# Scores of the next pair at the end of a pair's projection, and values turned in shared visits, in a decoder layer on one core

## The reference, cut to what matters

```python
def dilated_mixture_attention(h, w_in, w_out):
    qkv = (h @ w_in).reshape(B, S, 3, DSW_GROUPS, DSW_HEADS, DSW_HEAD_DIM)
    for g, (window, dilation) in enumerate(((128, 1), (512, 4), (2048, 16))):
        o, lse = dilated_window_attention(qkv[:, :, 0, g], qkv[:, :, 1, g], qkv[:, :, 2, g], window, dilation)
        outs.append(o); lses.append(lse)
    weights = jax.nn.softmax(jnp.stack(lses, axis=0), axis=0)
    o = jnp.sum(weights[..., None] * jnp.stack(outs, axis=0), axis=0)
    return o.reshape(B, S, D_MODEL).astype(h.dtype) @ w_out
```

## Time and profile before

| | us |
|---|---|
| median of 3 runs | 953.76 (953.18 to 954.54) |
| profiled execution, its own time | 953.11 |
| its span, first to last instruction | 951.3 |
| PE busy in the span | 927.2 (97%) |
| DVE, ACT busy | 577.5 (61%), 446.5 (47%) |

### The profile page before, as it was taken

One profiled execution on the slowest core, in us unless ns is written; L12 is line 12 of the kernel. 1 busy time (PEld: TensorE's weight loads), 2 busy tenths in 40 slices (PEclk: granted clock), 3 DMA queues, 4 the chain that ended last, 5 costly groups with the idle time before them and its releaser, 6 DMA issues.

```text
span 951.3 us, 16326 instructions
## 1 busy us (share of the span) xinstructions
PE 927.2 (97%) x5828; PEld 798.7 (84%) x5828; DVE 577.5 (61%) x1269; ACT 446.5 (47%) x804; POOL 51.2 (5%) x75
## 2 busy tenths in 40 slices
PE   7999999999999999999999899999999999999996
PEld 6688888888888888888888689889999999888884
DVE  3445655636736557357374757788888888733325
ACT  7244534435444445363443454655665665523222
POOL 2000000000000000000000001411211111000000
PEclk9999999999999999999999999999999999999998
DMA  9866341443324324334143112367877886432302
GB/s 305 252 184 170 111 133 47 131 133 110 122 76 132 110 69 128 112 110 154 45 133 96 38 53 81 104 155 176 185 184 180 178 196 146 156 110 89 110 1 89
DMA packets 166516, 121.19 MB, mean 127 GB/s; under 512 B 4662, under 2 KB 149198, under 8 KB 166478
## 3 DMA queue, kind: packets, MB, share of 16 engines
q1 hardware_dynamic: 161088, 111.17, 38.9%
q0 software_dynamic: 5184, 9.44, 6.6%
q10 hardware_dynamic: 206, 0.08, 0.0%
HBM read 109.13 MB, written 2.10 MB: 117 GB/s over the span
## 4 chain that ended last, share of the span: by engine, by line
PE 89%; DVE 5%; ACT 2%; POOL 1%; DMA 1%; issue 1%; SPq 1%; DVEq 0%; ACTq 0%
PE bank L778 14%; PE bank L780 13%; PE bank L779 13%; PE bank L983 7%; PE bank L986 7%; PE bank L985 7%; PE bank L1032 4%; PE bank L1033 4%; PE bank L1034 4%; PE bank L860 3%; PE bank L836 3%; PE bank L803 1%; PE bank L796 1%; PE bank L818 1%; PE bank L869 1%; PE bank L871 1%
## 5 line engine op out<-in xcount | busy, mean ns | idle before, releaser
L1379 DVE TENSOR_TENSOR wl<-raw,wh 128x1024 fp32r<-128x1024 f32 (+1 forms) x127 | 150.2, 1183 | 166.2 <-ACT wh L1090 165.6
L778 PE MATMUL bank<-hh,wl 128*128 128x512 f32 x544 | 218.1, 401 | 0.0
L780 PE MATMUL bank<-hl,wh 128*128 128x512 f32 x544 | 212.4, 390 | 0.0
L779 PE MATMUL bank<-hh,wh 128*128 128x512 f32 x544 | 212.0, 390 | 0.0
L1090 ACT ACTIVATE wh<-raw 128x1024 fp32r<-128x1024 f32 (+1 forms) x127 | 130.4, 1028 | 61.4 <-PE bank L1034 50.2
L778 PEld LDWEIGHTS bank<-hh,wl 128*128 128x128 f32 x544 | 102.3, 188 | 23.9 <-issue 3.5
L780 PEld LDWEIGHTS bank<-hl,wh 128*128 128x128 f32 x544 | 102.1, 188 | 22.2
L779 PEld LDWEIGHTS bank<-hh,wh 128*128 128x128 f32 x544 | 102.3, 188 | 19.5
L1161 ACT ACTIVATE probs<-probs,nmax 128x256 f32<-128x256 f32 (+1 forms) x128 | 61.8, 484 | 67.5 <-DVE nmax L1455 67.5
L983 PE MATMUL bank<-th,wl 128*128 128x256 f32 x304 | 86.2, 284 | 1.6 <-ACT p_copy L1247 0.9
L986 PE MATMUL bank<-tl,wh 128*128 128x256 f32 x304 | 86.0, 283 | 0.0
(11 more groups left out here) (220 smaller groups left out, 1609.2 us busy)
## 6 DMA issues: line engine op xcount, KB each, us to landing
raw<-in_attn_w_in SPq DMA_DIRECT2D x72, 512.0 KB, 3.8
ada_raw<-in_w_ada SPq DMA_DIRECT2D x16, 1024.0 KB, 6.1
raw<-in_ffn_w_up SPq DMA_DIRECT2D x25, 512.0 KB, 4.2
sums<-in_ffn_w_up SPq DMA_DIRECT2D x36, 256.0 KB, 3.4
raw<-in_ffn_w_down SPq DMA_DIRECT2D x17, 512.0 KB, 3.3
sums<-raw POOLq DMA_DIRECT2D x27, 256.0 KB, 4.8
ada<-in_w_ada SPq DMA_DIRECT2D x16, 256.0 KB, 6.6
raw<-in_attn_w_out SPq DMA_DIRECT2D x8, 512.0 KB, 3.6
```

The lines of the kernel that those rows point to most:

```text
L778: nc.tensor.matmul(bank[:], wl[:, slot, t], xh[:, t], start=(t == 0), stop=False)
L779: nc.tensor.matmul(bank[:], wh[:, slot, t], xh[:, t], start=False, stop=False)
L780: last = nc.tensor.matmul(bank[:], wh[:, slot, t], xl[:, t], start=False, stop=(t == KT - 1))
L1379: nc.vector.tensor_tensor(dst, src, high.bitcast(F32), ALU.subtract).then_inc(done, 1)
```

## The change

Four things are moved; no arithmetic is added or taken away.

- Scores 0 and 1 of a pair go from h 0 of the body that attends to it to h 16 of the body that projects it, behind the values of the pair before. Their masks and exponentials go to h 16 and 17. On ACT the copy `o_a` goes ahead of them.
- Values: turn 0 and turn 1 at h 4, just ahead of scores 2 and 3, turn 2 at h 12 ahead of the sum. The first pair keeps its own table.
- In body 8 only scores 2 and 3 are left, at h 1 instead of 4, with their masks and exponentials at h 1 and 2.
- The filling steps of body 8 are spread anew: 3 and 18 at h 0 and 1 instead of 5 and 15 at h 0 and 4, and 3 instead of 4 at h 16.

The semaphore of scores 0 asks only for strips up to 4 of its pair, that of scores 2 for all.

```diff
-        SCORE_AT = {0: (0, 1), 4: (2, 3)}
-        MASK_AT = {0: 0, 1: 1, 4: 2, 5: 3}
-        TURN_V_AT = {3: 0, 5: 1, 7: 2}
+        SCORE_AT = {4: (2, 3)}
+        SCORE_LAST = {1: (2, 3)}
+        SCORE_AHEAD = {16: (0, 1)}
+        MASK_AT = {4: 2, 5: 3}
+        MASK_LAST = {1: 2, 2: 3}
+        MASK_AHEAD = {16: 0, 17: 1}
+        TURN_V_AT = {4: (0, 1), 12: (2,)}
...
-        FILL_AT = {0: 5, 4: 15, 12: 1, 13: 1, 14: 1, 15: 1, 16: 4}
+        FILL_AT = {0: 3, 1: 18, 12: 1, 13: 1, 14: 1, 15: 1, 16: 3}
...
                 if d == 0:
+                    pe.wait_ge(strip_taken, STRIPS * (n - 1) + GROUPS + 2)
+                if d == 2:
                     pe.wait_ge(strip_taken, STRIPS * n)
...
+                    if project:
+                        for d in SCORE_AHEAD.get(h, ()):
+                            make_scores(n + 1, par, d)
...
+                    if project and h in MASK_AHEAD:
+                        if attend and h == 16:
+                            copy_output(n)
+                        exponentials(n + 1, MASK_AHEAD[h])
                 if attend:
-                    act.wait_ge(pv_done, 4 * n)
-                    nc.scalar.activation(o_a[:].rearrange("p (b j r) -> p b j r", b=NT, r=4),
-                                         o_acc[0][:].rearrange("p (b r j) -> p b j r", b=NT, r=4),
-                                         ACT.Copy).then_inc(oa_copied, 1)
+                    if not project:
+                        copy_output(n)
                     act.wait_ge(o_summed, n + 1)
...
+                    if project and h in MASK_AHEAD:
+                        mask_scores(n + 1, MASK_AHEAD[h])
```

More of the change, by code:

```diff
@@ L259, in decoder_layer @@
         HALVES = 2 * STRIPS
-        TURN_V_FIRST = {8: 0, 9: 1, 10: 2}
+        TURN_V_FIRST = {8: (0,), 9: (1,), 10: (2,)}
         ADA_READ_FIRST = {4: 0, 5: 1, 6: 2, 7: 3, 12: 4, 13: 5, 14: 6, 15: 7}
         ADA_FIRST = 17
-        FILL_AT = {0: 5, 4: 15, 12: 1, 13: 1, 14: 1, 15: 1, 16: 4}
+        FILL_AT = {0: 3, 1: 18, 12: 1, 13: 1, 14: 1, 15: 1, 16: 3}
         OUT_AHEAD = 4
@@ L905, in body @@
                     if project:
-                        g = STRIPS * n + s
+                        at = STRIPS * n + s
                         if h % 2 == 0:
-                            pe.wait_ge(l_ready, g + 1)
-                            pe.wait_ge(strip_taken, s - RING if is_first(n) and s < FIRST + 2 else g - 1)
+                            pe.wait_ge(l_ready, at + 1)
+                            pe.wait_ge(strip_taken, s - RING if is_first(n) and s < FIRST + 2 else at - 1)
                         last = half_strip(qkv_bank(n, par, s), qkv_slot(n, s), h % 2, hh, hl)
@@ L913, in body @@
                         turn_v_at = TURN_V_FIRST if is_first(n) else TURN_V_AT
-                        if h in turn_v_at:
-                            turn_values(n, par, turn_v_at[h])
+                        for g in turn_v_at.get(h, ()):
+                            turn_values(n, par, g)
                         if h == (ADA_FIRST if is_first(n) else ADA_AT):
@@ L918, in body @@
                     if attend:
-                        if h in SCORE_AT:
-                            for d in SCORE_AT[h]:
-                                make_scores(n, 1 - par, d)
+                        for d in (SCORE_AT if project else SCORE_LAST).get(h, ()):
+                            make_scores(n, 1 - par, d)
                         for j in PV_AT.get(h, ()):
@@ L1130, in take_probs, with exponentials, copy_output @@
                 nc.scalar.activation(p_t[:, u % PT_RING], turn_bank(u, project)[:], ACT.Copy).then_inc(p_taken[1], 1)
+            def exponentials(n, d):
+                act.wait_ge(nmax_done, 4 * (n - 1) + d + 1)
+                side = d // 2
+                for b in (2 * (d % 2), 2 * (d % 2) + 1):
+                    for hd in range(2):
+                        tile = probs[:, hd, side, b, (P if d == 0 and b == 0 else 0):HALF]
+                        last = nc.scalar.activation(tile, tile, ACT.Exp, bias=nmax[:, side, b, hd:hd + 1],
+                                                    scale=SCORE_SCALE, accum_out=stat[:, side, b, 1, hd:hd + 1])
+                last.then_inc(exp_done, 1)
+            def copy_output(n):
+                act.wait_ge(pv_done, 4 * n)
+                nc.scalar.activation(o_a[:].rearrange("p (b j r) -> p b j r", b=NT, r=4),
+                                     o_acc[0][:].rearrange("p (b r j) -> p b j r", b=NT, r=4),
+                                     ACT.Copy).then_inc(oa_copied, 1)
             def body(n, par, project, attend):
@@ L1146, in body @@
                             nc.scalar.activation(dst, src, ACT.Copy).then_inc(strip_taken, 1)
-                        if (TURN_V_FIRST if is_first(n) else TURN_V_AT).get(h) == 1:
+                        if 1 in (TURN_V_FIRST if is_first(n) else TURN_V_AT).get(h, ()):
                             act.wait_ge(v_turned[1], n + 1)
@@ L1153, in body @@
                     if attend:
[L1154 to L1163, removed]
+                        d = (MASK_AT if project else MASK_LAST).get(h)
+                        if d is not None:
+                            exponentials(n, d)
                         if h == 8:
@@ L1491, in body @@
                                                     ).then_inc(ada_taken, 1)
-                        g = (TURN_V_FIRST if is_first(n) else TURN_V_AT).get(h)
-                        if g in (0, 2):
-                            take_values(n, g, v_n[:, par, g].rearrange("p b e -> p (b e)"))
+                        for g in (TURN_V_FIRST if is_first(n) else TURN_V_AT).get(h, ()):
+                            if g != 1:
+                                take_values(n, g, v_n[:, par, g].rearrange("p b e -> p (b e)"))
                     if attend:
-                        if h in MASK_AT:
-                            mask_scores(n, MASK_AT[h])
+                        d = (MASK_AT if project else MASK_LAST).get(h)
+                        if d is not None:
+                            mask_scores(n, d)
                         if h == 8:
```

## The result

The change made the kernel slower: 961.41 us (median of 6, 958.92 to 963.91) against 954.15 (median of 6, 951.63 to 954.69) beside it on the same chip. The ratio is 1.0076 [1.0064, 1.0088]. Forecast were 950.8 and a gain. The profiled execution took 961.12 us, its span is 959.3, so 8.0 us more than the 951.3 of before.

What follows compares the result with a forecast made beforehand. PE's own queue was taken to bound the kernel. Turns 1.05, scores behind values 1.4 and tail 0.5 summed to 2.95 us, from the median 953.76 to 950.8 us; range 948.5 to 952.8.

Steps and rivals of the forecast that it cites:

- What bounds the kernel: Attention loop: PE has 90.00 us of work in 90 us, so only what leaves PE's queue gains time.
- Turns of values: Half strips 4 and 12: three visits fewer a pair save 0.15 us, over seven pairs 1.05 us.
- Rival 1: PE's visits: only changes of tile shape cost, so the turns give nothing; gain 1.9 us, 951.9 us; chance 0.15.
- Scores behind the values: Half strip 16: joining both visits saves one shape change, 0.23 us a pair, 1.4 us over six pairs.
- The middle of a pair on DVE and ACT: Middle pairs: moved masks and exponentials cost nothing, with 4.3 us or more to spare before PE waits.
- rival 4: Half strip 2: exponentials ahead of strip 8's copy hold PE in each of eight rounds; 4.0 us lost, 955.3; chance 0.05.
- rival 3: Loop's gain doesn't reach the end, or tile to tile costs two changes and turns nothing; 0.5 us or less, 953.3; chance 0.10.
- The tail: Last body: the order of work on ACT and DVE lets the moved work gain only 0.5 us.
- the walk's 0.5: Last body, followed step by step on ACT and DVE: swap starts at 537.3 instead of 537.79, 0.5 us earlier.
- the new one for ol: Last body, behind the last values: with three filling steps instead of four, PE waits 0.6 us for ol.
- Rival 2: Last body: ol and the split don't delay the third mask, so the tail gains 2.5 us; 948.8 us; chance 0.12.
- the term for round 1 in the sum: Body 0: round 1's scores make a visit of their own there, so moving them gives none of the 1.4 us.

Runs made afterwards that it cites:

- t_unroll: Kernel before with only the turns of values moved as in the change and PE's loop written out: 951.61 us, 0.9965 of the kernel before.
- s_unroll: Kernel before with only the scores, their tables and the last body's filling steps changed, PE's loop written out: 951.51 us, 0.9974 of the kernel before.
- a_tail2: Changed kernel, PE's loop written out; in the last body DVE does ol behind the third mask and its fourth-strip split later: 947.81 us, 0.9936 of the kernel before.
- a_hold28: Changed kernel, loop kept, 28 instead of 44 throw-away transposes at PE's start, so the loop begins at instruction 928 again: 950.78 us, 0.9956 of the kernel before.
- a_pad64: Changed kernel with 64 more instructions without work (128 waits) ahead of PE's loop: 956.14 us, 1.0023 of the kernel before.
- b_pad96: Kernel before with 96 more instructions without work (192 waits) ahead of PE's loop: 960.94 us, 1.0069 of the kernel before.
- b_hold60: Kernel before with 60 instead of 44 throw-away transposes at PE's start, 32 more instructions ahead of its loop: 968.01 us, 1.0143 of the kernel before.
- a_unroll: Changed kernel with PE's loop over the pairs written out, nothing else: 949.71 us, 0.9953 of the kernel before.
- b_unroll: Kernel before with PE's loop over the pairs written out, nothing else: 953.74 us, 0.9992 of the kernel before.
- a_tail2_h28: Changed kernel with the DVE order of a_tail2, but PE's loop kept and 28 throw-away transposes at the start: 947.88 us, 0.9939 of the kernel before.

## Why the prediction was wrong

**What bounds the kernel.** Right. PE's queue set the bodies, and what was taken off it came out in the distance from values to values, to 0.03 us of the forecast 0.38.

**Turns of values.** Forecast 0.15 a pair, measured 0.11 (t_unroll); the bounds 0.6 to 2.1 us for seven pairs hold 0.8. The sign named for it did not come: the visit at half strip 4 was to be 0.1 shorter than its parts. The scores' visit alone before, then the joined one of t_unroll:

```profile
227.76 0.39 PE L780 MATMUL bank<-hl,wh 128*128 128x512 f32 x1
228.08 2.06 PE L803 MATMUL bank<-k_t,q_t 64*128 64x128 f32 x32
...
230.41 0.39 PE L779 MATMUL bank<-hh,wh 128*128 128x512 f32 x1
```

```profile
226.77 0.40 PE L792 MATMUL bank<-hl,wh 128*128 128x512 f32 x1
227.01 1.08 PE L830 MATMUL bank<-ident,v_t 128*128 128x128 f32 x8
228.02 2.06 PE L815 MATMUL bank<-k_t,q_t 64*128 64x128 f32 x32
...
230.34 0.39 PE L791 MATMUL bank<-hh,wh 128*128 128x512 f32 x1
```

Less two steps that is 2.20 before, with two turns of 0.46 and 0.48 beside it 3.13, and joined 3.12; the other visit gains 0.02. So some 0.03 of the 0.11 are in the visits. The rest is in the matmuls behind them: behind a visit the steps up to the next lose 0.02 to 0.04 in all, and there are three visits fewer. Rival 1, that turns give nothing, falls: a visit costs something without a change of shape too. The rule of the Trainium skill that the prediction weighed (TensorEngine Tiling (Array Packing), Key Properties) tells where PEld stands, and isn't the whole cost.

**Scores behind the values.** Forecast 0.23 a pair, measured 0.24 (s_unroll). The joined visit in body 2 runs from L784 at 206.30 to L783 at 210.58:

```profile
206.30 0.39 PE L784 MATMUL bank<-hl,wh 128*128 128x512 f32 x1
206.62 1.97 PE L866 MATMUL bank<-p_t,v_n 128*64 128x128 f32 x32
208.52 1.79 PE L802 MATMUL bank<-k_t,q_t 64*128 64x128 f32 x16
210.24 0.50 PE L782 MATMUL bank<-hh,wl 128*128 128x512 f32 x1
210.58 0.40 PE L783 MATMUL bank<-hh,wh 128*128 128x512 f32 x1
```

PEld at the same place:

```profile
208.52 1.39 PEld L802 LDWEIGHTS bank<-k_t,q_t 64*128 64x128 f32 x16 [0.17 <-issue]
```

4.28 less two steps (0.453) is 3.83; its content is 1.72 + 1.505 = 3.225, so 0.60 is fixed. That is the 0.38 and 0.41 of the earlier trace rows less 0.19: from tile shape to tile shape costs one change, not two and not none. The weight load stands 0.17 us there, as the earlier trace rows has it between values and turned probabilities. The forecast 2.10 + 1.75 us for this visit met 3.83.

**The middle of a pair on DVE and ACT.** No wait of PE for k_t or wl in the loop, as forecast; rival 4 had no part in the loss. With PE's loop at its old place or written out the gain of the bodies reached the end, so rival 3 falls too.

**The tail.** In the changed kernel swap starts at 544.26, 27.07 behind the body's values at 517.19; before, 537.79 - 510.12 = 27.67. So the walk's 0.5 us was 0.6, no wait for k_t is left, the one for p_t is still 2.60, and the new one for ol is 0.52 where 0.6 was forecast. Rival 2 named the mechanism that a_tail2 used: with ol out of the third mask's way, and the split behind the masks, the wait falls by 1.6.

**The step that failed** is the term for round 1 in the sum: "round 1 gives none, since its scores now make a visit of their own in body 0". It puts the move into body 0 at nothing and prices moved instructions only by the time in which they run. The change takes the eight matmuls of round 1 to body 0, ahead of PE's loop; that this moves the loop's code I didn't ask, and the queue of instruction transfers on the page I didn't read. In place of nothing the runs show a fetch of nine packets at each of two jumps, 5.95 and 3.47 us: 9.4 us, three times the whole forecast gain. No rival held it: rival 4, the slower one, sat on ACT and ended at 955.3, and the range at 952.8. Without the stalls the forecast holds: a_hold28, the same change with the loop's code at its old place, took 0.9956 [0.9940, 0.9973] of before, and the forecast gain of 2.95 us is 0.9969.

What is shown: that 32 instructions ahead of the loop make the stalls in either order of the work, that 32 fewer or 64 more take them away, and that nine transfers of 16 KB go with each stall and none with a free jump. Why the limit lies just there is argued. From 84 to 213 us, bodies 1 and 2, the instruction queue moves 6 packets in the kernel before, a_hold28, a_pad64 and b_pad96, and 8 in the changed kernel and b_hold60; of those 8 the last two, at 208.6 and 210.8 in the changed kernel, start just ahead of the stall. One of them fits a loop that touches one block of code more from its new place, the other a first fetch for the jump. By the 12 packets for 3,144 instructions a block is some 240 to 260 instructions, an estimate, so the loop is six blocks long or a little more, and whether it touches one more or one less depends on where it begins. The loop that touches one less would stay, the other not.

The Trainium skill (Runtime: NRT & Kernel Launch, Instruction fetch mechanics) gives PE room for 2,048 instructions, refilled in blocks of 256, and says that a taken branch whose target isn't in the current window of two blocks waits for a fetch.
## What to carry to other kernels

Where an engine runs a loop in the program, count what moves across the loop's edge, not only what moves in it: compare the engine's instructions ahead of the loop before and after, and read the instruction queue's packets in the profile. "issue" in front of a plain matmul just behind a jump, with more instruction packets, was code being fetched in every profile here; shift the loop, or write it out, before the change is judged. In a tail whose engines work in order, move what stands in the way of the critical step behind it on that engine alone, and leave the step that feeds it early on the other engine.

## What the runs showed that I had not expected

- A jump back was free in one place and cost 2.97 to 5.27 us in another, 32 instructions on. With the slow clock behind it one jump cost up to 7.8 us.
- Of the four stalls in the profiles of the changed kernel and b_hold60, the clock fell to the lower level behind three (2.97, 5.27 and 4.49 us), and not behind the one of 3.27. In all four PE goes on 1.3 to 1.4 us behind the end of the third of the packets around the jump (the one that starts at 213.8 in the first stall of the changed kernel).
- It also falls in the tail behind the wait of 2.6 us for p_t, with or without the loop's stalls. Of the changed order, a_hold28 has it and a_unroll doesn't; of the old order, b_unroll has it and the profiled run of before doesn't. The two stretches of 5 us from that wait's end, a_unroll and a_hold28:

```profile
545.24:550.24 5.00, 5.00 (x50) 4.23 (x51) 1.38 (x2) 1.09 (x2) 0.00 (x0) 1.00 0.01 3
```

```profile
544.27:549.27 5.00, 5.00 (x40) 4.17 (x40) 0.69 (x1) 0.60 (x1) 0.00 (x0) 0.66 0.02 3
```

  So the +1.39 in the table of the result isn't the change's. Each kernel has one profile, but every run has its mean granted clock, and in the kernel before the two go together: in the three comparisons its 14 runs at 0.997 took 952.16 to 953.64 us, its 26 at 0.993 to 0.996 took 953.71 to 955.99. In both profiles with the wait cut to 0.99 us the slow stretch is absent; two profiles don't prove that the shorter wait keeps it away. What a_tail2_h28 gains over a_hold28 can't be split further: it is 2.9 us by medians from two comparisons and 1.6 by their ratios.
- Waits that hold nothing up any more aren't free on PE: 192 of them put the start off by 8.6 us and 128 by 5.2, so 64 more cost 3.45 us, 0.054 each.
